# Eighteen more of each part's 128 dot products ahead of the index scores in VectorE's program order

## The reference

```
def peer_ffn(h, w_q, sub_keys, exp_u, exp_v):
...
        top_s, pos = lax.top_k(cand, PEER_TOPK)
        e = jnp.take_along_axis(cand_idx, pos, axis=-1)
        g = jax.nn.softmax(top_s, axis=-1)
        u = exp_u[e]
        act = jax.nn.gelu(jnp.einsum('btd,bthkd->bthk', xb.astype(F32), u.astype(F32)), approximate=False)
        coef = (g * act).astype(xb.dtype)
        vv = exp_v[e]
        return jnp.einsum('bthk,bthkd->btd', coef, vv)
```

## Time and profile before

| What | Value |
|---|---|
| median of 3 runs | 1929.71 us (1923.74 to 1929.81) |
| the profiled execution | 1930.05 us, its span 1927.8 us |
| VectorE busy | 1015.4 us, 53% |
| GpSimd busy | 992.1 us, 51% |
| TensorE busy | 1098.2 us, 57% |
| bytes moved | 696.06 MB, mean 361 GB/s |
| gathers (software queue) | 538.24 MB |
| weights and the rest (hardware queue) | 156.58 MB |

### The profile page before, as it was taken

The page is one execution under the profiler, slowest core; times in us unless marked ns, Lnnn a source line. Parts: engine busy times, 40 slices in busy tenths (PEclk is TensorE's granted clock), DMA queues, the critical chain, the costliest instruction groups (busy, mean ns, idle before and its releaser), DMA issues.

```text
span 1927.8 us, 19711 instructions
## 1 busy us (share of the span) xinstructions
PE 1098.2 (57%) x7062; PEld 631.2 (33%) x7062; DVE 1015.4 (53%) x2647; ACT 297.4 (15%) x842; POOL 992.1 (51%) x1072
## 2 busy tenths in 40 slices
PE   5997887757167555858066555948167550003554
PEld 4764655444034114544044114634044110000110
DVE  1142287679736406687826307687836309994000
ACT  2342112342000002451010002442010000000000
POOL 2000007335555776344654776334655777776774
PEclk9997877876579787987588887977678675556888
DMA  8646599968999999998999999988999999999998
GB/s 300 210 158 241 207 325 398 400 249 329 404 407 398 404 410 407 391 347 313 406 406 402 383 409 406 395 294 297 405 406 369 378 409 410 410 410 409 409 409 324
DMA packets 230913, 696.06 MB, mean 361 GB/s; under 512 B 23958, under 2 KB 23974, under 8 KB 230818
## 3 DMA queue, kind: packets, MB, share of 16 engines
q0 software_dynamic: 148080, 538.24, 71.5%
q1 hardware_dynamic: 82738, 156.58, 22.5%
HBM read 693.70 MB, written 1.05 MB: 360 GB/s over the span
## 4 chain that ended last, share of the span: by engine, by line
DMA 34%; PE 19%; POOL 13%; DVE 12%; issue 6%; ACT 3%; POOLq 0%; ACTq 0%; DVEq 0%
DMA rows<-in_peer_v,v_at 16%; DMA rows<-in_peer_u,u_at 11%; POOL rows L489 8%; DMA wring<-in_w_in 7%; PE ps L623 6%; DVE rows L1016 6%; PE ps L582 5%; POOL rows L481 5%; PE ps L571 3%; PE ps L540 2%; ACT diag_eq L843 1%; PE ps L604 1%; PE ps L520 1%; PE ps L698 1%; ACT hT L809 1%
## 5 line engine op out<-in xcount | busy, mean ns | idle before, releaser
L481 POOL DMA_INDIRECT rows<-in_peer_u,u_at x512 | 483.0, 943 | 661.0 <-DVE dots L1016 284.5
L1016 DVE CUSTOM_DVE_ANT_0 rows<-rows,ps 128x1024 f32<-128x1024 f32 x512 | 605.8, 1219 | 216.4 <-DMA rows<-in_peer_u,u_at 205.4
L489 POOL DMA_INDIRECT rows<-in_peer_v,v_at x512 | 497.7, 972 | 253.3 <-issue 131.9
L623 PE MATMUL ps<-rows,spread_c 128*32 128x512 f32 x2048 | 343.2, 804 | 272.4 <-DMA rows<-in_peer_v,v_at 272.4
L623 PEld LDWEIGHTS ps<-rows,spread_c 128*32 128x32 f32 x2048 | 74.4, 131 | 513.1 <-issue 511.5
L571 PE MATMUL ps<-wring,hT 128*128 128x512 f32 x384 | 191.3, 654 | 43.7 <-DMA wring<-in_w_in 32.5
L582 PE MATMUL ps<-hT,wring 128*128 128x128 f32 x1536 | 186.3, 285 | 15.3 <-ACTq L813 13.2
L582 PEld LDWEIGHTS ps<-hT,wring 128*128 128x128 f32 x1536 | 183.4, 201 | 24.0 <-ACTq L813 18.8
L520 PE MATMUL ps<-ident,coef 128*128 128x128 f32 x4 | 1.9, 476 | 325.2 <-DVE coef L1261 325.2
L843 ACT ACTIVATE diag_eq<-ident,cwT 128x128 f32<-128x128 f32 x496 | 148.4, 387 | 35.2 <-PE ps L604 33.3
L571 PEld LDWEIGHTS ps<-wring,hT 128*128 128x128 f32 x384 | 78.3, 211 | 143.9 <-issue 90.0
(11 more groups left out here) (192 smaller groups left out, 910.8 us busy)
## 6 DMA issues: line engine op xcount, KB each, us to landing
wring<-in_w_ada SPq DMA_DIRECT2D x48, 1024.0 KB, 8.7
wring<-in_w_in SPq DMA_DIRECT2D x48, 1024.0 KB, 14.6
wring<-in_peer_wq SPq DMA_DIRECT2D x32, 1024.0 KB, 16.4
wring<-in_w_out SPq DMA_DIRECT2D x16, 1024.0 KB, 10.7
rows<-in_peer_u,u_at POOLq DMA_INDIRECT x512, 11.9
rows<-in_peer_v,v_at POOLq DMA_INDIRECT x512, 9.1
wring<-in_w_in SPq DMA_DIRECT2D x4, 288.0 KB, 23.1
out_x<-xs SPq DMA_DIRECT2D x2, 512.0 KB, 4.6
```

The source lines that it names most:

```text
L481: pool.indirect_dma_start(row(n), None, u_rows, bass.IndirectOffsetOnAxis(ap=u_at[:, p % 2, k:k + 1], axis=0)).then_inc(row_landed[n % SLO ...
L489: pool.indirect_dma_start(row(n), None, v_rows, bass.IndirectOffsetOnAxis(ap=v_at[:, p % 2, tok:tok + 1], axis=0)).then_inc(row_landed[n % ...
L623: ins = pe.matmul(ps[32 * g:32 * g + 32, YB + q, :], spread_c[:, g, a, :], row(n)[:, q * 512:q * 512 + 512], start=a == 0, stop=a == 31)
L1016: dve.tensor_tensor_reduce(out=row(n), in0=row(n), in1=h2_shown, scale=1.0, scalar=0.0, op0=ALU.mult, op1=ALU.add, accum_out=dots[:, k:k + ...
```

## The change

Four of the counts in `first(p)` grow, by 2, 4, 6 and 6, all of them ahead of `index_scores`. The counts behind it stay. `coefficients` does what is left of the 128, so it has 18 fewer: 37 instead of 55 in part 1, 40 instead of 58 in part 2, 34 instead of 52 in part 3. The number of dots, gathers and loads is the same, and so is the order on TensorE, ScalarE, GpSimd and SyncE. In `first(0)` there are no dots.

```
@@ -1080,14 +1080,14 @@
                 seq_(ts(hb[:, :], xs[:, t, :], rs[:, 0:1], None, ALU.mult), h_ready)
-                more_dots(14)
+                more_dots(16)
                 dve.wait_ge(sig_ready, p + 1)
...
                 dve.sem_inc(glu_done, 1)
-                more_dots(10)
+                more_dots(14)
...
@@ -1103,7 +1103,7 @@
                 seq_(dve.tensor_copy(pjh[:, 25, :], pjh[:, 24, :]), idx_ready)
-                more_dots(14)
+                more_dots(20)
...
@@ -1115,7 +1115,7 @@
                 seq_(rotate(t, 0, 16), qk_ready)
-                more_dots(8)
+                more_dots(14)
 
                 index_scores(l, t)
                 more_dots(2)
```

## The result

The changed kernel takes 1897.23 us, the median of 4 runs (1896.08 to 1898.18), against 1928.99 us for the kernel before (1923.74 to 1929.81): a ratio of 0.9841, 95% interval 0.9822 to 0.9859. That is faster by 1.6%, 31.8 us where 28.6 were forecast. The profiled execution took 1897.10 us, 32.9 less than the one of before.

A forecast was written before the change was run, and what follows sets the result against it. Transfers bound the kernel, plus idle DMA time behind the start of the index scores. Gains of 10.0, 9.3 and 9.3 us, together 28.6, took 1930.05 to 1901.4, stated as 1901 us; range 1882 to 1932.

The forecast's parts named there:

- What bounds the kernel: From the first gather: bytes over rate, plus idle DMA time behind the scores' start, 27, 17 and 25 us by part.
- terms of the sum: Per part, 23.0 us less the scores' delay: 10.0 in part 1, 9.3 each in parts 2 and 3, together 28.6 us.
- What the tail gives back: Between attention and coefficients: 18 rows fewer at 1.28 us, 23.0 us per part, the tail staying bound by transfers.
- The delay of the scores: Index scores start later, the later of two ways counting: VectorE's dots or the weights; 13 us part 1, 13.7 parts 2, 3.
- the weights' 15.4: Part 1 ahead of the scores: 12 rows ahead of v's last block take 15.4 us; averaged with 10.5 to 13.
- part 2 by VectorE: Ahead of part 2's scores: rows from the 14th dot on come every 2.04 us, so scores start 13.7 us later.
- part 2 by the weights: Rows ahead of v's last block in part 2 cost 7.7 to 15.4 us, mean 11.6, below 13.7, changing nothing.
- The time to landing: Part 2's run of 20 dots: rows land 12.3 us after the gather, so the 14th dot's row comes about 806.4.
- Reckoning in order of issue: Without packet-by-packet queue sharing, 12 rows precede every v block: delay 15.4 throughout, sum 3 x 7.6 = 23 us.
- A: Rival: ahead of the scores only VectorE's overrun delays, 5.8 us; each part gains 17.2, in all 52: 1878 us. Chance 0.15.
- B: Rival: the idle DMA hole behind the scores' start only moves; delay 23.0 us, time stays at 1930. Chance 0.10.
- C: Rival: VectorE starves for rows ahead of and behind the scores, 2.62 us a row, deciding pace 2.51; 1960 us. Chance 0.12.

The follow-up runs named there:

- second condition: Four follow-up batches, each on another chip: unedited kernel before takes 2053 to 2072 us; the change itself there 2051.12 us against 2053.23, ratio 0.9987.
- first condition: The condition of the first result, chip not known: kernel before 1928.99 us, changed kernel 1897.23 us; no experiment met it.

## Why the prediction was right, and where it wasn't

**What bounds the kernel: right for the first result.** Transfers ahead of the scores and in the tail, idle DMA time between. The gain of the parts, 26.2 us, is about the fall of the idle DMA time, 27 us. In the second condition this doesn't hold ahead of the scores: the kernel before moves only 359 to 370 GB/s there, where it moved 396 to 400.

**The total: nearer than its terms.** The terms of the sum gave 28.6 us, and the three parts that they describe gained 26.2. The 31.8 us of the result come out only with what lies outside the parts, 6.7 us between the two profiles, which the prediction put at nothing and no run explains. That the total is only 3 us off is luck in part.

**What the tail gives back: right.** 18 x 1.28 = 23.0 us was the term; 22.1, 23.1 and 22.4 were measured, and 23.5 to 24.9 in the second condition. That the tail is the rows' and not VectorE's was shown in the second condition by the run with short dots there; in the first the tail's DMA share of 1.03 says so for part 1.

**The delay of the scores: the sum right, its two ways mixed up.** Part 1: 13 forecast, 11.3 measured. Part 2: 13.7 and 14.2. Part 3: "its delay is taken as that of part 2", 13.7, and it was 16.4. The prediction gave the weights a say in part 1 and VectorE the last word in parts 2 and 3. The profile shows it the other way round. In part 1 TensorE's index products are no later at all (102.9 us after the norm before and after), and its waits for `in_w_in` are as long as they were. VectorE's way, rows at steps of 2.04 us, sets the delay alone: the 10.5 us of that way were nearly right, and the mean with the weights' 15.4 spoiled it. In part 2 the last of the 34 dots did wait for its row (0.70 us) and the scores began 1.5 us after it, as the step "part 2 by VectorE" has it. But the step "part 2 by the weights", which I set aside as changing nothing, gives the delay as well: L1111 came 11.9 us later by the k projection, about the 11.6 of that step, and the index products 14.2 later, so by these marks the scores would have come no sooner without VectorE's dots. In part 3 VectorE waited 5.10 us for the relu at the scores, so there TensorE's way alone set the delay, a little over the 15.4 us that I gave as its bound. The waits for `in_w_in` are 11.4 us longer there, and the L571 products took 5.8 us longer. That the three delays are near the forecast although their causes are dealt out otherwise is luck too. The row of part 3 in the profile after:

```profile
1257.83 0.35 DVE L1053 TENSOR_SCALAR mixed_use<-mixed_use,wis 128x256 f32<-128x256 f32 x1 [5.10 <-ACTq L888]
```

**The time to landing: a little small, and it didn't matter.** I took 12.3 us for the rows of the run of 20 in part 2. In the kernel after, between 776 and 800 us, where this run stands, it was 15.5 us. It depends on the stretch: between 345 and 362 us, in part 1, it was 16.8 before and 23.6 after. Yet the first wait for a row in part 2 came at the 18th dot of the 20 and not at the 15th: the 14th row, whose gather was issued at 781.31, was there when its dot began at 794.66, and the next few came faster than every 2.04 us. The last of the 34 began 105.4 us after the norm, where the forecast has its row at 105.2. Queues and rows of part 1 between 345 and 362 us, then the rows of part 2 between 776 and 800:

```profile
q0 software_dynamic: 1207, 4.38, 65.6%
q1 hardware_dynamic: 1209, 2.41, 37.5%
...
rows<-in_peer_u,u_at POOLq DMA_INDIRECT x10, 23.6
...
rows<-in_peer_u,u_at POOLq DMA_INDIRECT x15, 15.5
```

The first two rows are the shares of the two queues in that stretch: packet for packet, as the earlier trace rows and as the rule of the Trainium skill (DMA: Bandwidth & Descriptors, "Queues, rings and completion order") has it. Reckoning in order of issue would have given 23 us; the parts gained 26.2, which lies between that and the 28.6 of the forecast, so the gain doesn't tell the two apart.

**The rivals.** A (the full gain, 52 us) did not come: no part had a delay near 5.8 us. B, the hole that only moves, is wrong for the first result and right for the second condition, and so is its number: the delay of the scores is 21 to 27 us there, around the 23 at which nothing is gained, and the idle time of the hole is the same to within 1 us before and after. Its cause is another than B names, TensorE's issue time. C, starving for rows, was named for VectorE at 2.51 us a row; where dot after dot waited for its row, as from 402.97 to 409.08 us in part 1, the step was about 2.04. (C's "never exceed 0.82 us" holds but for one dot, which waited 1.84 us just behind the norm, at 295.74.) In the second condition it is TensorE that is held up, which I had not thought of. The forecast's chance of 0.78 for "faster" would have been too high for the second condition.

## What to carry to other kernels

When the DMA engines are the bound nearly everywhere, look for the stretches where they idle, and ask of a moved transfer two things: how much it shortens the place that it leaves (here 1.28 us a row), and how much later it makes the first step that everything else waits for. The gain is the difference, and it is no more than the idle time there is. And check which engine is the last to reach that step in each part: here it was another one in part 1 than in part 3. Measure such a change on more than one chip: the same 18 moves gained 1.6% under one condition and nothing under another, though each half of the account could be read from the marks in both.

## What the runs showed of the hardware that I had not expected

Under the second condition TensorE slows down beside a stream of gathered rows. While rows alone filled the DMA engines its products came one in 1.4 to 2.8 us, from about the 47th product on. In the first condition the same instructions run back to back beside the same stream, for instance from 304 to 310 us, when this moved:

```profile
q0 software_dynamic: 657, 2.40, 100.0%
```

The profile calls this issue and names no releaser. The run without dots at the first place shows that the gaps move with the rows, from L582 to L604. A slower supply of instructions while the DMA engines are full would look like this, but that is a guess: no run took the instructions' own transfers away, and why the first result doesn't show it is open. The DMA queues of the changed kernel in that stretch, 300 to 325 us, second condition:

```profile
q0 software_dynamic: 2799, 10.20, 102.3%
q8 instruction: 1, 0.02, 0.3%
```

10.20 MB of rows in 25 us are 408 GB/s, and no weight moves at all; by the kernel's order a load waits there until TensorE is done with a block of the weight ring.

These gaps aren't all of the second condition either. Between the profiles of the kernel before in the two conditions lie 132 us; the three parts, from norm to coefficients, are 60 of them, and 72 lie elsewhere. The dots of part 3's experts have no work of TensorE beside them, and there too the second condition moves less. The kernel before in the first condition, then in the second:

```profile
1700.00:1756.00 56.00, 0.00 (x0) 0.00 (x0) 53.24 (x88) 0.31 (x1) 42.29 (x46) 0.50 1.03 410
1800.00:1874.00 74.00, 0.00 (x0) 0.00 (x0) 62.62 (x106) 0.11 (x1) 49.72 (x54) 0.50 0.99 370
```

410 against 370 GB/s, with TensorE idle in both. So the rows come more slowly there without any part of TensorE; why, no run tells.
